# Nine small scale/shift groups, spread key/value tiles and later splits at the start of a two-block kernel

## The chip, the cores and the metric

The kernel runs on one core of one Trainium2 chip. The metric is the device time of one execution in microseconds; a kernel's time is the median of its runs. The engines are named PE (TensorE; PEld is its weight load), ACT (ScalarE), DVE (VectorE), POOL (GpSimd) and SP (SyncE, which issues every DMA here).

## What is computed

Two transformer blocks over 256 tokens of width 2048, all in float32. Only the start of the first matters for the change:

```python
shift, scale, gate = split(silu_c @ w_ada + b_ada, 3)        # w_ada is 2048 x 6144
shift_c, scale_c, _ = split(silu_cc @ w_ada + b_ada, 3)
h  = rmsnorm(x,   norm_g) * (1 + scale)   + shift            # 256 tokens
hc = rmsnorm(ctx, norm_g) * (1 + scale_c) + shift_c          # 256 context tokens
kc, vc = hc @ w_in[:, K and V columns]                       # 8 tiles of 128 columns
p  = h @ w_in                                                # all columns, K and V among them
...                                                          # attention, Fourier mix, merge, second block
```

Every later step needs `h`, and `h` needs the scale and shift rows, which need 4096 columns of `w_ada` (32 MB).

## The kernel before

All operands are feature-major: 16 feature tiles (kt) of 128 partitions, tokens along the free axis. A product of a weight tile with an operand is made of three matmuls in fp32r: the weight is split into a rounded part (`whi`, made by ACT) and the rest (`wlo`, made by DVE), the operand likewise (`act` holds both parts).

Engine queues are recorded by a planner. `Queue.put` adds an instruction and moves the queue's planned time; jobs (generators, in `jobs`) are advanced by `step()` whenever PE's planned time passes the time at which what they wait for is expected, plus `MARGIN`. So the order on ACT and DVE is fixed at build time by planned costs. On the chip only semaphores count, and every engine works its own queue in order.

The work is a `stream` of items, and `flow()` walks it: loads are issued `LOADS` = 8 items ahead into `NR` = 7 raw buffers of 512 KB (SP's DMAs, in stream order; a buffer is loaded again once its last reader is done), weights are split `AHEAD` = 3 items ahead (`prepare`), and then the item's matmuls are put (`piece`). Kinds of item in the start:

- S, a scale/shift tile of `w_ada` (`s_group`, `s_pe`): 512 KB, read raw by four small matmuls of 32 x 256, in the four column groups of PE, with `CW` (the two silu vectors) as weights. Two sections (scale, shift) of a group share one PSUM bank, `s_bank`.
- B, a piece of the first seven of the eight key and value tiles (`together`, `run_group`): some of the seven units, for the feature tiles of one group; `whi`/`wlo` are split from it. Each unit holds a PSUM bank through the whole start, so seven of the eight banks are held, and `s_bank` has the eighth.

`GROUPS` cuts the 16 feature tiles into five groups of 2, 4, 4, 4, 2. When the last S item of a group is through, the job `s_cols` copies the bank (ACT), sums the four row groups with 128x2 matmuls on PE, makes the modulation columns in `mod` (DVE), gives the bank back, and goes on into `h_group`, which makes the operands `act` of the group's feature tiles on ACT and DVE; only then can B items of that group run. A group of n tiles has 16 S items for n = 4 and 8 for n = 2; `S_PLACE` says behind which S items the B items stand. Fifteen of 18 B items stand between S items, three behind them. Then come the eighth value tile (`v7`, two items of kind G), and 24 query and gate tiles and so on, for 2.65 ms.

Before S items, `squares` puts 16 matmuls of ones with x squared, and `norm_in` makes the inverse root from them.

Of the kernel before, what the change touches and what calls it, by code (L numbers as in the profile page):

```python
# [21 lines left out]
S_PLACE = (1, 3), (1, 6), (1, 9), (2, 4), (2, 7), (2, 10), (2, 13), (3, 4), (3, 7), (3, 10), (3, 13), (4, 4), (4, 6), (4, 7), (4, 7)  # L22
KV_FIRST = 7
S_COST = 0.15
# [3 lines left out]
MARGIN = 1.2  # L28
AHEAD = 3
# [89 lines left out]
def block_kernel(nc, src, out):  # L119
# [164 lines left out]

    def hop(tokens):

        if expected(tokens) > PE.time + 0.05:
            yield [(c, v, when - MARGIN) for c, v, when in tokens]

# [66 lines left out]
    def step():  # L356

        moved = False
        for j in list(jobs):
            if j[1] <= PE.time:  # L360
                try:
                    toks = next(j[0])
                    j[1] = expected(toks) + MARGIN if toks else PE.time
                    moved = moved or bool(toks)
                except StopIteration:
                    jobs.remove(j)
                    moved = True
        return moved
# [122 lines left out]
    state = {}  # L491
# [91 lines left out]

    def flow():
        n = len(stream)
        at = 0
        for i in range(-LOADS, n):
# [9 lines left out]
            if 0 <= i + AHEAD < n:  # L597
                prepare(i + AHEAD)
# [33 lines left out]
    GROUPS = ((0, 2), (2, 4), (6, 4), (10, 4), (14, 2))  # L632

    def s_pe(it):
# [3 lines left out]
        n = GROUPS[j][1]  # L638
# [4 lines left out]
        o = bank[:, 256 * sec:256 * sec + 256]  # L643
        w = RAW[it["raw"] % NR]
        PE.wait(it["in"])
        for q in range(4):
            k = q if n == 2 else q // 2
            last = mm(o[32 * q:32 * q + 32, :], CW[:, kts[k], :], w[:, 256 * q:256 * q + 256], kts[0] == 0, kts[-1] == 15,
                      tell=q == 3, cost=S_COST)
# [4 lines left out]
    def s_cols(j, bank, tok):  # L654
# [3 lines left out]
        t = copy(rows[:, :], bank[:, :], tok + f)  # L658
        yield t
        PE.wait(t)  # L660
        for sec in range(2):
            for b in range(n):
                x, sel = (b, 0) if n == 2 else (b % 2, 1 + b // 2)
                at = 2 * (n * sec + b)
                last = mm(bank[:, at:at + 2], rows[:, 256 * sec + 128 * x:256 * sec + 128 * x + 128], col(C_SEL + 2 * sel, 2),
                          True, True, tell=sec == 1 and b == n - 1)
# [499 lines left out]
    def s_group(j):  # L1166
# [7 lines left out]
                       {2: (3, 1, 3), 4: (2, 2, 1, 2)})  # L1174
# [11 lines left out]
    HALVES = (8, 8)  # L1186
    for i in range(KV_FIRST, 8):
# [827 lines left out]
def _lay_out(x):  # L2015
# [36 lines left out]
    for q in range(4):  # L2052
        for at in (C_SEL, C_SEL + 2 + 2 * (q % 2)):
            cols[32 * q:32 * q + 2, at:at + 2] = np.eye(2)
# [20 lines left out]
```

How the kernel before makes its waits and increments, by code:

```python
    def put(self, fn, needs, tell=True, cost=0.1):  # L72
        self.wait(needs)
        self.time += cost
        if not tell:
            self.ops.append(fn)
            return None
        count = self.done
        self.ops.append(lambda e: fn(e).then_inc(count.handle, 1))
        return count.add(1, self.time + self.tail)
# [5 lines left out]
    def play(self, e):  # L86
        for op in self.ops:
            if isinstance(op, tuple):
                e.wait_ge(op[0].handle, op[1])
            else:
                op(e)
# [183 lines left out]
    def dma(o, i, count, needs=(), q=None):  # L275
        q = q or SP
        q.wait(needs)
        q.ops.append(lambda e: e.dma_start(o, i).then_inc(count.handle, 16))
        q.time += max(0.65, size(o) * 4 * 128 / 335e3)
        return count.add(16, q.time + 2.0)
```

## Time and profile before

| | us |
|---|---|
| median of 3 runs | 2834.73 (2834.42 to 2835.02) |
| the profiled execution | 2834.52 |
| its span in the profile | 2832.7 |
| PE busy | 2773.2 (98%) |
| DVE busy | 2077.2 (73%) |
| ACT busy | 1475.7 (52%) |
| HBM read | 612.69 MB, 218 GB/s over the span |

The span is the time from the first to the last instruction that the profiler saw; the device time has 1.8 us more. "Busy" for PE means that a matmul is under way; at half the granted clock a busy PE does half the work. The granted clock is 1.00 at 2.4 GHz and 0.50 at 1.2 GHz. Chain lines, waits and timelines name an instruction by engine, line and tile; buffer numbers are left out, and `[x <-y]` at the end of a line is x us of idle time before it, ended by y.

### The profile page before, as it was taken

What the parts mean: (1) busy time and instruction counts of PE and PEld (TensorE: products, weight loads), DVE (VectorE), ACT (ScalarE), POOL (GpSimd) and SP (SyncE); (2) the same over time, 40 slices, a digit from 0 to 9 for tenths busy, and PEclk for the clock granted to TensorE, in tenths of its full rate; (3) what the DMA queues carried; (4) which work ended last, traced back from release to release, by engine and by line L of the source; (5) the groups of instructions that cost most, each with busy time, mean ns of one, the idle gap of its engine ahead of it and who ended that gap; (6) DMA issues with size and microseconds to landing.
All of it is one profiled execution on the core that took longest, in us unless ns stands there. A gap on an engine that the chain in (4) does not pass through costs nothing. (4 is left out here: it accounts for less than half of the span.)

```text
span 2832.7 us, 43001 instructions
## 1 busy us (share of the span) xinstructions
PE 2773.2 (98%) x16104; PEld 2390.9 (84%) x16104; DVE 2077.2 (73%) x3551; ACT 1475.7 (52%) x2394; POOL 339.6 (12%) x1005
## 2 busy tenths in 40 slices
PE   7899999999989999999999999999989999999999
PEld 3578888888878888888888888888878888888888
DVE  2368877888887888887787877888878765566654
ACT  2265554555557667666666644545444543344443
POOL 0004420000003152423324210000000000000000
PEclk8999999999999999999999999999999999999999
DMA  8866667888955555555555578788768766655554
GB/s 307 287 199 225 212 207 250 284 269 287 314 158 205 175 173 184 168 185 182 171 176 167 169 263 284 252 291 297 251 196 280 246 186 187 193 190 188 185 186 148
DMA packets 196626, 621.82 MB, mean 220 GB/s; under 512 B 20273, under 2 KB 38721, under 8 KB 195649
## 3 DMA queue, kind: packets, MB, share of 16 engines
q1 hardware_dynamic: 196416, 619.08, 66.8%
q8 instruction: 126, 2.06, 0.3%
q14 instruction: 84, 0.68, 0.1%
HBM read 612.69 MB, written 4.21 MB: 218 GB/s over the span
## 5 line engine op out<-in xcount | busy, mean ns | idle before, releaser
L266 PE MATMUL ps<-act,whi 128*128 128x512 f32 x6560 | 1756.8, 399 | 30.3 <-DVE act L261 21.8
L251 DVE TENSOR_TENSOR wlo<-raw,whi 128x1024 fp32r<-128x1024 f32 (+2 forms) x885 | 1045.6, 1186 | 453.3 <-ACT whi L242 252.7
L266 PEld LDWEIGHTS ps<-act,whi 128*128 128x128 f32 x6560 | 1168.5, 189 | 248.0 <-issue 26.8
L242 ACT ACTIVATE whi<-raw 128x1024 fp32r<-128x1024 f32 (+2 forms) x885 | 881.3, 1022 | 210.8 <-PE ps L266 151.0
L266 PE MATMUL ps<-act,wlo 128*128 128x256 f32 (+1 forms) x6416 | 981.4, 287 | 2.3 <-DVE wlo L251 2.3
L266 PEld LDWEIGHTS ps<-act,wlo 128*128 128x128 f32 x6416 | 895.8, 190 | 73.5 <-DVE wlo L251 5.1
L242 ACT ACTIVATE t<-ps 128x256 f32<-128x256 f32 (+2 forms) x393 | 147.9, 377 | 478.3 <-PE ps L266 429.8
L261 DVE SCALAR_TENSOR_TENSOR acc<-raw,c_act,acc 128x1024 f32<-128x1024 f32 x210 | 267.8, 1277 | 0.0
L242 ACT ACTIVATE t<-t 128x256 f32<-128x256 f32 (+3 forms) x261 | 115.5, 443 | 193.5 <-DVE t L251 162.4
L251 POOL TENSOR_TENSOR small<-small 128x2 f32<-128x2 f32 (+2 forms) x460 | 167.0, 363 | 231.3 <-ACT t L242 138.7
L251 DVE TENSOR_TENSOR t<-t,ps 128x256 f32<-128x256 f32 (+2 forms) x391 | 153.8, 394 | 28.1 <-ACT t L242 25.2
L257 POOL TENSOR_SCALAR small<-small 128x2 f32<-128x2 f32 (+3 forms) x256 | 91.1, 356 | 629.2 <-DVE small L257 609.4
L261 DVE SCALAR_TENSOR_TENSOR t<-t,t 128x256 f32<-128x256 f32 (+2 forms) x160 | 70.9, 446 | 25.7 <-ACT t L242 24.2
L266 PE MATMUL ps<-m_act,whi 128*128 128x512 f32 x256 | 64.2, 392 | 0.4 <-ACT whi L242 0.4
L251 POOL TENSOR_TENSOR small<-small,small 128x4 f32<-128x4 f32 (+1 forms) x160 | 57.1, 357 | 13.1
L1443 POOL MEMSET t<- 128x4 f32 x31 | 2.8, 101 | 454.1 <-PE ps L266 420.7
L261 DVE SCALAR_TENSOR_TENSOR h_res<-ps,mod,h_res 128x256 f32<-128x256 f32 x64 | 31.0, 484 | 34.9 <-PE ps L266 33.8
L242 ACT ACTIVATE act<-t 128x256 fp32r<-128x256 f32 x48 | 20.0, 416 | 68.1 <-DVE t L251 68.1
L266 PEld LDWEIGHTS ps<-t,t 128*128 128x128 f32 x286 | 48.4, 189 | 6.8
L266 PE MATMUL ps<-t,t 128*128 128x128 f32 (+1 forms) x286 | 53.9, 281 | 0.0
L266 PEld LDWEIGHTS ps<-m_act,whi 128*128 128x128 f32 x256 | 46.1, 189 | 9.0 <-ACT whi L242 0.6
L251 DVE TENSOR_TENSOR t<-t,t 128x256 f32<-128x256 f32 (+1 forms) x104 | 47.7, 459 | 4.3 <-ACT t L242 1.1
(208 smaller groups left out, 1873.0 us busy)
## 6 DMA issues: line engine op xcount, KB each, us to landing
raw<-in_w SPq DMA_DIRECT2D x427, 512.0 KB, 5.0
raw<-in_w_mod SPq DMA_DIRECT2D x192, 512.0 KB, 4.8
raw<-in_w_ada SPq DMA_DIRECT2D x96, 512.0 KB, 6.4
raw<-in_w_gate SPq DMA_DIRECT2D x88, 512.0 KB, 4.7
raw<-in_w_up SPq DMA_DIRECT2D x88, 512.0 KB, 4.7
raw<-in_w_out SPq DMA_DIRECT2D x64, 512.0 KB, 5.8
raw<-in_w_down SPq DMA_DIRECT2D x64, 448.0 KB, 3.7
raw<-in_p_a SPq DMA_DIRECT2D x32, 512.0 KB, 5.7
```

The source lines that it names most:

```text
L242: return AC.put(lambda e: e.activation(o, i, func, **kw), needs, cost=cost)
L251: return (q or DV).put(lambda e: e.tensor_tensor(o, a, b, op), needs, cost=max(0.4, size(o) * 0.0036) if q else 0.07 + size(o) * 0.00104)
L257: return (q or DV).put(lambda e: e.tensor_scalar(o, a, s1, s2, op0, op1), needs, cost=cost)
L261: return DV.put(lambda e: e.scalar_tensor_tensor(o, a, s, b, op0, op1, **kw), needs, cost=0.07 + size(o) * 0.00104 + 0.06 * column(s))
L266: return PE.put(lambda e: e.matmul(o, w, x, start=start, stop=stop), needs, tell, cost)
L1443: z = GP.put(lambda e: e.memset(xp[:, 0:4], 0.0), f)
```

## The change

1. `GROUPS` has nine groups: two of one feature tile, seven of two. An S item of a one-tile group holds 8 row blocks of 128 columns (512 B runs in HBM) and is read by eight matmuls of 32 x 128; of a two-tile group, 4 row blocks of 256 columns (1 KB runs). The four-tile groups before had 512 columns (2 KB runs). The number of S items stays 64.
2. The B items are 16: one of 7 units in each one-tile group, and two of 4 and 3 units in the others. Their runs are 512 B or 1 KB (1 KB or 2 KB before). `S_PLACE` puts a group's two B items behind the fifth and eighth S item of the group after it; the last two stand behind all S items.
3. In the start a B item is split no earlier than one item ahead of its matmuls (`hasty`), unless the planner expects it to have landed and a `wlo` buffer to be free (`early`). Behind the start (`end_start`) the rule is the old one.
4. Until `end_start` the planner's margin is 0.3 instead of 1.2.
5. `s_cols` copies only the filled part of the bank; the selector columns `C_SEL` lose two variants that the four-tile groups needed.

```diff
-S_PLACE = (1, 3), (1, 6), (1, 9), (2, 4), (2, 7), (2, 10), (2, 13), (3, 4), (3, 7), (3, 10), (3, 13), (4, 4), (4, 6), (4, 7), (4, 7)
+S_PLACE = [(1, 3), (2, 7)] + [(j, p) for j in range(3, 9) for p in (4, 7)]
...
+FIRST_MARGIN = 0.3
...
-            yield [(c, v, when - MARGIN) for c, v, when in tokens]
+            yield [(c, v, when - spare[0]) for c, v, when in tokens]
...
-                    j[1] = expected(toks) + MARGIN if toks else PE.time
+                    j[1] = expected(toks) + spare[0] if toks else PE.time
...
+    def hasty(i, k):
+
+        return state["start"] and k > max(i, 0) + 1 and stream[k]["kind"] == "B"
+
+    def early(it):
+
+        if it["kind"] == "B":
+            return expected(it["in"]) <= PE.time and (ring["hi"] < NL or ("lo", ring["hi"] - NL) in pe_free)
+        return it["kind"] == "S"
...
-            if 0 <= i + AHEAD < n:
-                prepare(i + AHEAD)
+            while after < n and (after <= i + AHEAD and not hasty(i, after) or after < at and early(stream[after])):
+                prepare(after)
+                after += 1
...
-    GROUPS = ((0, 2), (2, 4), (6, 4), (10, 4), (14, 2))
+    GROUPS = [(0, 1), (1, 1)] + [(k, 2) for k in range(2, 16, 2)]
...
-        for q in range(4):
-            k = q if n == 2 else q // 2
-            last = mm(o[32 * q:32 * q + 32, :], CW[:, kts[k], :], w[:, 256 * q:256 * q + 256], kts[0] == 0, kts[-1] == 15,
-                      tell=q == 3, cost=S_COST)
+        for k, kt in enumerate(kts):
+            q = kt % 4
+            last = mm(bank[32 * q:32 * q + 32, c * sec:c * sec + c], CW[:, kt, :], w[:, c * k:c * k + c], kt < 4, kt >= 12,
+                      tell=kt == kts[-1], cost=c / 2330)
...
-        t = copy(rows[:, :], bank[:, :], tok + f)
+        t = copy(rows[:, 0:256 * n], bank[:, 0:256 * n], tok + f)
...
-                       {2: (3, 1, 3), 4: (2, 2, 1, 2)})
+                       {1: (7,), 2: (4, 3)})
...
+    def end_start():
+        spare[0] = MARGIN
+        state["start"] = False
+
+    add({"kind": "X", "run": end_start})
```

On ACT, before: from the column copy of the first group (out of `ps1`) to that of the second (out of `ps2`). `whi` rows are splits of B items, `act` and `t1` rows are `h_group`.

```order
L242 ACTIVATE t2_1_139<-ps1 128x512
L242 ACTIVATE whi0_56<-raw5_54 128x768
L242 ACTIVATE act_65<-xc_66,mod_97 128x256
L242 ACTIVATE t1_1_155<-xc_66,mod_97 128x256
L242 ACTIVATE act_65<-xc_66,mod_97 128x256 x2
L242 ACTIVATE t1_3_157<-xc_66,mod_97 128x256
L242 ACTIVATE act_65<-xc_66,mod_97 128x256
L242 ACTIVATE whi1_57<-raw2_51 128x256
L242 ACTIVATE whi2_58<-raw6_55 128x768
L242 ACTIVATE t2_2_140<-ps2 128x512
```

ACT now, from the copy of the third group to that of the fourth:

```order
L242 ACTIVATE t2_3_141<-ps2 128x512
L242 ACTIVATE act_65<-xc_66,mod_97 128x256
L242 ACTIVATE t1_5_159<-xc_66,mod_97 128x256
L242 ACTIVATE act_65<-xc_66,mod_97 128x256 x2
L242 ACTIVATE t1_7_161<-xc_66,mod_97 128x256
L242 ACTIVATE act_65<-xc_66,mod_97 128x256
L242 ACTIVATE whi2_58<-raw2_51 128x1024
L242 ACTIVATE whi3_59<-raw6_55 128x768
L242 ACTIVATE t2_4_142<-ps2 128x512
```

The operands of a group now stand directly behind its column copy, and the splits behind them; both splits of a group still stand ahead of the next copy.

On PE, before, at the end of the third group (the last matmuls of a B piece, the last two S items, the column sums with `cols`, the first S items of the fourth group; `c_wide` is `CW`):

```order
L266 MATMUL ps1<-act_65,whi1_57 128x512 x2
L266 MATMUL ps1<-act_65,wlo2_63 128x512
L266 MATMUL ps2<-raw3_52,c_wide_92 32x256 x4
L266 MATMUL ps2<-raw4_53,c_wide_92 32x256 x4
L266 MATMUL ps2<-cols_96,t2_3_141 128x2 x8
L266 MATMUL ps2<-raw5_54,c_wide_92 32x256 x4
L266 MATMUL ps2<-raw6_55,c_wide_92 32x256 x4
```

PE now, at the end of the fourth group (feature tiles 4 and 5):

```order
L266 MATMUL ps2<-raw5_54,c_wide_92 32x256 x4
L266 MATMUL ps7<-act_65,whi3_59 128x512 x2
L266 MATMUL ps7<-act_65,wlo3_64 128x512
L266 MATMUL ps7<-act_65,whi3_59 128x512 x2
L266 MATMUL ps7<-act_65,wlo3_64 128x512
L266 MATMUL ps2<-cols_96,t2_4_142 128x2 x4
L266 MATMUL ps0<-act_65,whi3_59 128x512 x2
L266 MATMUL ps0<-act_65,wlo3_64 128x512
```

The column sums stood between S items and now stand inside the B piece of three units, behind its first unit.

## Rows read from the trace of the kernel before

**Rows 1.** The page, part 2: granted clock in tenths, 40 slices.

```profile
PEclk8999999999999999999999999999999999999999
```

**Rows 2.** Busy times by stage: window, length, PE, PEld, DVE, ACT, POOL busy, clock, DMA share, GB/s.

```profile
0.00:183.08 183.08, 152.63 (x948) 99.22 (x949) 64.20 (x144) 60.37 (x104) 0.73 (x5) 0.91 0.81 278
183.08:2832.70 2649.62, 2620.57 (x15157) 2291.71 (x15155) 2012.98 (x3409) 1415.30 (x2291) 338.92 (x1000) 1.00 0.66 215
```

**Rows 3.** Timeline of PE: start, us, what; squares, last S item, first of v7.

```profile
8.32 16.41 PE L266 MATMUL ps<-t,k 128*128 128x512 f32 x32 [8.32 <-ACT t L242]
...
161.97 0.64 PE L266 MATMUL ps<-raw,c_wide 128*32 128x256 f32 x8
...
183.08 1.30 PE L266 MATMUL ps<-act,whi 128*128 128x512 f32 x5
```

**Rows 4.** Timeline of PE: a first product at half clock, S items, products, ones.

```profile
42.07 1.19 PE L266 MATMUL ps<-act,whi 128*128 128x512 f32 x2 [4.42 <-DVE act L251]
...
48.93 1.50 PE L266 MATMUL ps<-raw,c_wide 128*32 128x256 f32 x24
50.36 0.73 PE L266 MATMUL ps<-act,whi 128*128 128x512 f32 x2
...
77.24 0.62 PE L266 MATMUL ps<-act,whi 128*128 128x512 f32 x2
...
77.93 0.62 PE L266 MATMUL ps<-act,whi 128*128 128x512 f32 x2
...
175.88 1.02 PE L266 MATMUL ps<-t,k 128*128 128x512 f32 x2
```

**Rows 5.** Timeline of PE at the end of the third group.

```profile
101.67 1.95 PE L266 MATMUL ps<-cols,t 128*128 128x2 f32 x16 [0.72 <-ACT t L242]
104.72 3.92 PE L266 MATMUL ps<-raw,c_wide 128*32 128x256 f32 x40 [1.10 <-DVE mod L251]
```

**Rows 6.** Busy times in windows of 2 us, before and at a fall of the clock.

```profile
60.00:62.00 2.00, 0.85 (x16) 0.16 (x8) 0.00 (x0) 0.00 (x0) 0.00 (x0) 1.00 1.05 398
...
64.00:66.00 2.00, 1.78 (x9) 1.78 (x10) 0.00 (x0) 0.17 (x1) 0.00 (x0) 0.60 1.06 389
```

**Rows 7.** The same windows where the queues are full or empty.

```profile
10.00:12.00 2.00, 2.00 (x4) 0.78 (x3) 0.69 (x1) 1.15 (x2) 0.00 (x0) 1.00 1.03 434
12.00:14.00 2.00, 2.00 (x5) 0.92 (x4) 0.69 (x1) 0.33 (x1) 0.00 (x0) 1.00 0.98 413
...
24.00:26.00 2.00, 2.00 (x29) 0.82 (x31) 0.69 (x1) 0.51 (x1) 0.00 (x0) 1.00 0.30 96
...
46.00:48.00 2.00, 2.00 (x8) 1.60 (x7) 0.14 (x1) 0.00 (x0) 0.00 (x0) 0.66 0.00 0
```

**Rows 8.** Waits of SP's queue in 0 to 200 us (us, times, longest); landing of raw tiles.

```profile
SPq L278 <- PE ps L266: 107.2, 47, 10.1
...
DMA to landing us min/median/max: 2.5/6.5/15.6
```

**Rows 9.** ACT's waits for landings; timeline of ACT and DVE around the first operands.

```profile
ACT whi L242 <- DMA raw<-in_w: 50.7, 11, 9.5
...
37.11 0.84 ACT L242 ACTIVATE whi<-raw 128x768 fp32r<-128x768 f32 x1 [6.84 <-DMA raw<-in_w]
...
38.93 0.15 DVE L251 TENSOR_TENSOR mod<-ps,cols 128x2 f32<-128x2 f32 x1
...
42.41 0.99 DVE L251 TENSOR_TENSOR act<-t,act 128x256 fp32r<-128x256 f32 x2 [0.49 <-ACT t L242]
```

**Rows 10.** Rates: 1 KB rows, 2 KB rows, and stretches with key/value loads.

```profile
16.00:24.00 8.00, 8.00 (x20) 3.60 (x19) 2.08 (x3) 2.54 (x3) 0.00 (x0) 1.00 1.10 348
62.00:68.00 6.00, 4.24 (x28) 3.51 (x24) 0.27 (x3) 0.60 (x1) 0.00 (x0) 0.70 1.05 388
90.00:104.00 14.00, 12.63 (x91) 8.85 (x89) 1.53 (x4) 1.65 (x2) 0.00 (x0) 1.00 0.98 348
126.00:130.00 4.00, 3.62 (x34) 2.13 (x32) 0.00 (x0) 1.00 (x1) 0.00 (x0) 1.00 0.95 262
126.00:142.00 16.00, 13.09 (x102) 9.18 (x104) 2.60 (x9) 2.33 (x4) 0.00 (x0) 1.00 1.02 320
```

More of the change, by code:

```diff
@@ L21 @@
 HEADS = 5
-S_PLACE = (1, 3), (1, 6), (1, 9), (2, 4), (2, 7), (2, 10), (2, 13), (3, 4), (3, 7), (3, 10), (3, 13), (4, 4), (4, 6), (4, 7), (4, 7)
+S_PLACE = [(1, 3), (2, 7)] + [(j, p) for j in range(3, 9) for p in (4, 7)]
 KV_FIRST = 7
-S_COST = 0.15
 V_LATE, Z_LATE = 1, 1
@@ L283, in lo_part @@
         return tt(o, full, hi.bitcast(F32), ALU.subtract, needs)
+    spare = [FIRST_MARGIN]
     def hop(tokens):
         if expected(tokens) > PE.time + 0.05:
-            yield [(c, v, when - MARGIN) for c, v, when in tokens]
+            yield [(c, v, when - spare[0]) for c, v, when in tokens]
     def split(kt, s, full, needs, scale=1.0):
@@ L489, in prepare @@
             state[key] = t + u
-    state = {}
+    state = {"start": True}
     def piece(it):
@@ L582, in run_group @@
         pe_free[("hi", n)] = pe_free[("lo", n)] = last
+    def hasty(i, k):
[4 more added lines that the diff above has]
+        return it["kind"] == "S"
     def flow():
         n = len(stream)
-        at = 0
+        at = after = 0
         for i in range(-LOADS, n):
@@ L629, in act_c @@
         t1.give(big, toks)
-    GROUPS = ((0, 2), (2, 4), (6, 4), (10, 4), (14, 2))
+    GROUPS = [(0, 1), (1, 1)] + [(k, 2) for k in range(2, 16, 2)]
     def s_pe(it):
         sec, j, kts = it["sec"], it["j"], it["kts"]
-        n = GROUPS[j][1]
+        c = 128 * GROUPS[j][1]
         if kts[0] == 0 and sec == 0:
@@ L642, in s_pe @@
         bank = state["s_bank"]
-        o = bank[:, 256 * sec:256 * sec + 256]
         w = RAW[it["raw"] % NR]
         PE.wait(it["in"])
-        for q in range(4):
-            k = q if n == 2 else q // 2
-            last = mm(o[32 * q:32 * q + 32, :], CW[:, kts[k], :], w[:, 256 * q:256 * q + 256], kts[0] == 0, kts[-1] == 15,
-                      tell=q == 3, cost=S_COST)
+        for k, kt in enumerate(kts):
+            q = kt % 4
+            last = mm(bank[32 * q:32 * q + 32, c * sec:c * sec + c], CW[:, kt, :], w[:, c * k:c * k + c], kt < 4, kt >= 12,
+                      tell=kt == kts[-1], cost=c / 2330)
         raw_free[it["raw"]] = state["acc", 0] = last
@@ L662, in s_cols @@
             for b in range(n):
[L663 to L666, printed above, removed]
+                x = n * sec + b
+                last = mm(bank[:, 2 * x:2 * x + 2], rows[:, 128 * x:128 * x + 128], col(C_SEL, 2), True, True,
+                          tell=sec == 1 and b == n - 1)
         t2.give(rows, last)
@@ L2052, in _lay_out @@
     for q in range(4):
-        for at in (C_SEL, C_SEL + 2 + 2 * (q % 2)):
-            cols[32 * q:32 * q + 2, at:at + 2] = np.eye(2)
+        cols[32 * q:32 * q + 2, C_SEL:C_SEL + 2] = np.eye(2)
     cols[:, C_EPS], cols[:, C_E2] = EPS, EPS * EPS
```

## The prediction

> **What bounds the kernel now.** First the page: TensorE is busy in 98% of the span, and the only one of 40 slices in which its granted clock is below nine tenths is the first [rows 1]. Then the busy times by stage: I cut at 183.08 us, where the first matmuls of the eighth value tile (v7) start, since the edited part of the program ends there [rows 2, 3]. Up to that cut PE is idle for 183.08 − 152.63 = 30.5 us, the granted clock is 0.91 and the queues move 278 GB/s; behind it PE is idle for 29 us in 2649.6, at clock 1.00. The end is therefore PE's: whatever the start gives back, the rest keeps, if its order stays. It does: after the start the engines' orders differ by a few interleaved rows only.
>
> What PE must do before the cut, at the full clock: until 24.66 us the load wait and the 32 squares matmuls; 64 scale/shift tiles at 0.48 us (three in 1.43, from 48.93 to 50.36); 112 tile products of keys and values at 0.684 us (spacing 77.24 to 77.93); column sums of 32 blocks, 8 take 1.95 us, so 7.8; two matmuls with ones, some 0.85 each, 1.7 [rows 3 to 5]. 24.7 + 30.7 + 76.6 + 7.8 + 1.7 = **141.5 us**. The other 42 us are 22 us of idle behind 8.32 and matmuls at the half clock. Where they are: at the end of each of the three big groups PE waits 0.72 us for ScalarE's copy of the columns, sums, and waits 1.10 us for VectorE's modulation columns, since seven of eight banks are held by key and value tiles and the next group's first matmul needs the eighth [rows 5]. Around that, tiles come one by one and the clock falls to 0.50 [rows 6]. While PE then runs a burst of key/value products, the 7 raw buffers are full and the queues stand still, 0 GB/s at 46 to 48 us [rows 7]; SyncE's queue waited 107.2 us for PE in the first 200 [rows 8]. And ScalarE blocks in its order on the split of a tile that has not landed: 6.84 us before 37.11, behind which stood the modulation that the operands needed (DVE 38.93) [rows 9].
>
> **The change, part by part.** I follow two floors, the queues' and PE's, to the moment at which v7 starts.
>
> *Row lengths.* The tile bytes stay the same: 64 × 512 KB, 7.34 MB of key/value weights, k1 0.92 MB. Their runs get shorter. Before: 10.2 MB in 1 KB rows, 30.7 MB in 2 KB rows. After: 5.11 MB in 512 B rows (8 tiles and 2 of 448 KB), 35.8 MB in 1 KB rows. Rates: x in 8 KB rows 413 to 434 GB/s; 1 KB rows 348; 2 KB rows 388 [rows 7, 10]. A row then takes one of 16 engines 47.1 ns for 1 KB and 84.5 for 2 KB, that is 9.7 + 37.4 per KB; for 512 B this gives 28.4 ns, 288 GB/s (an extrapolation; bounds 348, no penalty, and 174, same time per row). These are rates without key/value loads in the stream. With them 2 KB rows made 348 over 14 us, and a mixed stretch of mostly 1 KB rows 320 over 16 us, with 262 in its first 4 us, behind a key/value load [rows 10]. I take 320 for the mixed 1 KB stream.
>
> The Trainium skill, "DMA: Bandwidth & Descriptors", section Specifications, gives 512 B as the least transfer at line rate. By it the shorter rows would cost nothing; the rows above show 348 against 388 already from 2 KB to 1 KB, and nothing here shows 512 B. At 388 for all, the 129.5 us of the next paragraph would be 105.4.
>
> *Queue floor.* x is in at 14.0 us. 5.11 MB at 288: 17.7. 35.8 MB at 320: 111.8. k1 at about 430: 2.1. Sum 145.6. Behind the last scale/shift tile stand only 1.31 MB of key/value tiles and k1, 6.2 us, so that tile is transferred at 139.4 and landed at about 140.6 (the shortest way of a tile from issue to landing took 2.5 us, [rows 8], of which some 1.4 are its transfer). Holes: before, tile 8 could not be issued before PE was through the squares, a hole behind 24 us, 96 GB/s in the window [rows 7]; now the slower 512 B rows fill it (7 tiles take 12.7 us, to 26.7). One hole remains, I think: the first key/value piece cannot start before it is landed and split (about 33 us), runs some 7 us since the clock will have fallen, as it had by 42 us before, and holds all seven buffers: 2 us. Later groups: a period is 8 tiles and 7 tile columns × 2, 5.1 MB, 16 us at 320, against 8 × 0.48 + 0.95 + 14 × 0.684 = 14.4 us of PE. PE's longest piece is 8 products, 5.5 us, against 7 buffers, about 11 us. That is enough cover, with small holes of 0.3 us a group: 2 us in all. Last tile then at 144.6.
>
> *Tail.* From the last scale/shift matmul: 0.5; then the copy, 0.7, beside one unit of the 3-unit piece, 1.4 (the order rows on PE show it ahead of the sums), sums 0.95, modulation 0.9, and from there 3.7 us to the second tile of operands (39.7 to 43.4 before, [rows 9]): 7.0; then 13 products 8.9, ones 1.7: 18.1 us (20.6 before, from 162.5 to 183.08, [rows 3]). The piece of group 7 (4.1 us) lies beside the chain, as group 3's did. So v7 at 162.7 by the queues.
>
> *PE floor.* 141.5, plus 3.5 idle until the first piece, 2.5 before the second, 4 at half clock, 1 to 2 in the tail, 0.3 × 6: 155. The 0.72 and 1.10 us waits, and 1.95 of sums with nothing beside them, go: after the third group the sums stand inside a piece, and the bank is read long before the next group needs it. The four more column copies, 0.6 us each on ScalarE, are hidden: ScalarE is busy for 60 of 183 us [rows 2]. The 512 B tiles take 8 matmuls of 128 columns instead of 4 of 256: 0.48 to 0.96 us each, 0 to 4 us, hidden, since PE waits for loads there. PE joins at 155, the queues at 163, so the queues decide; I add 1.3 for half-clock stretches in which PE falls behind. **v7 at 164, 19.1 us earlier.**
>
> *Splits only once landed, margin 0.3.* They move 50.7 us of ScalarE waits for DMA [rows 9] behind the copies and operands. Worth what the chains above assume; by themselves nothing. What is late next is the last piece of each group: ScalarE still splits it ahead of the column copy (the order rows on ACT), and it lands 1.2 us after the last tile: up to 2 us a group when PE is level with the loads. With 2.5 us between chain and use I count none of it.
>
> *After the cut* nothing is added: ±2 us of interleaving.
>
> Total, against the profiled execution's own 2834.5: 2815.4. The median of the runs is 2834.73, 0.2 above, so **2815.6**. Faster or slower than 0.2% (5.7 us) is about what a measurement of this kernel can tell.
>
> **The rivals.**
> (A) The short rows cost little in the mixed stream (348, as without key/value loads; by the page's rule more still): 35.8 MB take 102.9 us, 9 less, and PE's 155 decides: 25 to 32 us gained, 2807. For it: 348 over 90 to 104 us with key/value loads, if in 2 KB rows. Against: 262 at 126 to 130, right behind a key/value load [rows 10].
> (B) PE's clock falls in each group. The tiles come 1.6 us apart for 0.48 us of work, and just such a stretch stood before the clock's fall at 64 us (0.85 us busy of 2 at 60 to 62, clock 0.60 at 64 to 66) [rows 6]. Each costs 2.3 us (4.7 us of work at half clock, from 42.07 to the middle of the window from 46 us, clock 0.66, [rows 4, 7]); seven of them 16, of which the 1.6 us of slack a group hides part: 7 to 12 us lost, gain 7 to 12, 2825. Against: PE is then late, has a backlog and runs without gaps. The Trainium skill, "TensorE: Matmul & The Clock Gate", section on HAM oscillation, tells of this: a wait for loads in each tile puts each tile at the half clock. By it this case would be the rule; here I see it as the second likeliest.
> (C) The change doesn't do what it says: the split is put where the planner expects the landing, at 335 GB/s, and the stream comes at 288 to 320. Then copy and operands wait behind it, 2 us × 7 = 14: gain 5, 2830.
> (D) Slower: the key/value loads in 1 KB rows hold the whole stream at the 262 GB/s of 126 to 130 us. 35.8 MB take 136.6 us, 24.8 more than I count: v7 at 189, 2840. It decides from 273 GB/s, where v7 stands at 183.
>
> **How the numbers follow.** Forecast (gain 13 to 25) 0.50, A 0.18, B 0.18, C 0.08, D 0.06. The range holds the forecast, A, and most of B: 2803 to 2827. Faster by over 0.2%: forecast, A and most of B, 0.83; within: C and the rest of B, 0.11; slower: D, 0.06.
>
> **What would show it.** v7's first matmul at 164 (155 for A, 174 for B). Rates of 340 to 350 (20 to 26 us in 512 B rows: 288) and no stretch at 0 GB/s after 45 us. No wait of PE for modulation columns after the second group. PE idle before the cut near 20 us. If v7 comes as said and the total does not, the rest of the order was not neutral; if 512 B rows run at 348, my line through two row lengths was wrong; if the clock is under 0.9 before the cut, B was right.

## The result and the profile after

| | before | after |
|---|---|---|
| median of 11 runs each, side by side (us) | 2835.59 (2833.14 to 2838.24) | 2828.92 (2826.89 to 2831.01) |
| profiled execution: span, its run (us) | 2832.7, 2834.5 | 2828.2, 2830.0 |
| v7's first matmul (us) | 183.08 | 176.57 |
| from there to the end of the span (us) | 2649.6 | 2651.6 |

The ratio is **0.9975, interval 0.9966 to 0.9984**: 6.7 us faster. The forecast was 19 us and a range from 2803 to 2827. The sign was right, the size a third of what I said, and the time is above my range. v7 should have started at 164.

On the page the busy share of TensorE is 98% as before, and the row of granted clocks is the same to the digit as in [rows 1]; at this grain the two kernels can't be told apart:

```profile
PE 2769.7 (98%) x16168; PEld 2393.1 (85%) x16168; DVE 2080.4 (74%) x3573; ACT 1477.8 (52%) x2396; POOL 339.3 (12%) x1005
PEclk8999999999999999999999999999999999999999
```

The busy times of the changed kernel, cut at v7's first matmul (columns as in [rows 2]; clock, DMA share and GB/s are the last three):

```profile
0.00:176.57 176.57, 145.89 (x1012) 98.89 (x1013) 66.76 (x161) 60.90 (x103) 0.73 (x5) 0.93 0.88 286
176.57:2828.20 2651.63, 2623.78 (x15157) 2294.16 (x15155) 2013.63 (x3413) 1416.89 (x2293) 338.55 (x1000) 1.00 0.66 215
```

TensorE's idle time ahead of the cut went from 30.5 to 30.7 us. What the change won there is busy time (152.6 us before, 145.9 now), and most of it is matmul time at the half clock: the granted clock stood at 0.50 for 34 of the 183 us before and for 24 of the 177 now, and busy time weighted by the granted clock, half-microsecond by half-microsecond, went only from 138.8 to 136.8 us. The timeline of TensorE tells where the idle time is now: the first matmuls of the first, second, fourth and following pieces, the last scale/shift tiles, the sums, the last piece, and v7:

```profile
35.92 1.19 PE L266 MATMUL ps<-act,whi 128*128 128x512 f32 x2 [3.45 <-DVE act L251]
48.50 0.64 PE L266 MATMUL ps<-raw,c_wide 128*32 128x256 f32 x8 [1.64 <-DMA raw<-in_w_ada]
52.55 1.19 PE L266 MATMUL ps<-act,whi 128*128 128x512 f32 x2 [3.41 <-ACT whi L242]
...
62.63 2.37 PE L266 MATMUL ps<-raw,c_wide 128*32 128x256 f32 x40
64.93 0.74 PE L266 MATMUL ps<-act,whi 128*128 128x512 f32 x2
...
81.18 0.70 PE L266 MATMUL ps<-act,whi 128*128 128x512 f32 x2 [1.07 <-ACT whi L242]
98.40 0.70 PE L266 MATMUL ps<-act,whi 128*128 128x512 f32 x2 [1.76 <-ACT whi L242]
114.39 0.70 PE L266 MATMUL ps<-act,whi 128*128 128x512 f32 x2 [0.53 <-ACT whi L242]
131.04 0.70 PE L266 MATMUL ps<-act,whi 128*128 128x512 f32 x2 [1.16 <-ACT whi L242]
148.95 0.70 PE L266 MATMUL ps<-act,whi 128*128 128x512 f32 x2 [0.85 <-ACT whi L242]
155.42 1.50 PE L266 MATMUL ps<-raw,c_wide 128*32 128x256 f32 x24
158.34 0.95 PE L266 MATMUL ps<-cols,t 128*128 128x2 f32 x8
164.37 0.70 PE L266 MATMUL ps<-act,whi 128*128 128x512 f32 x2 [2.24 <-ACT whi L242]
176.57 2.88 PE L266 MATMUL ps<-act,whi 128*128 128x512 f32 x12
```

The waits for column copies and modulation of [rows 5] are gone: the sums stand inside a piece and nothing waits for VectorE's columns. In their place TensorE waits for ScalarE's split at the first piece of every group. From the third piece (64.93) to the eighth group's first piece (148.95) a group takes 84.02 / 5 = **16.80 us**; the single groups take 16.25, 17.22, 15.99, 16.65 and 17.91 us, and in the last of them the granted clock was at 0.50 from 132.5 to 136.5 us. The third piece is late, too.

The queues in six stretches, one in 512 B rows, three in 1 KB rows, two in which next to nothing moves:

```profile
18.00:20.00 2.00, 2.00 (x6) 0.94 (x5) 0.69 (x1) 0.95 (x3) 0.00 (x0) 1.00 1.18 294
42.00:44.00 2.00, 2.00 (x16) 1.34 (x18) 1.63 (x3) 0.00 (x0) 0.00 (x0) 1.00 0.02 7
54.00:56.00 2.00, 2.00 (x7) 1.62 (x7) 0.00 (x0) 0.00 (x0) 0.00 (x0) 0.50 1.10 348
62.00:64.00 2.00, 2.00 (x32) 1.07 (x34) 2.00 (x3) 0.16 (x1) 0.00 (x0) 1.00 0.00 0
84.00:86.00 2.00, 2.00 (x11) 1.65 (x10) 0.00 (x0) 0.61 (x1) 0.00 (x0) 1.00 1.07 355
88.00:90.00 2.00, 2.00 (x28) 1.20 (x18) 0.00 (x0) 0.60 (x1) 0.00 (x0) 1.00 0.63 175
```

Where nothing holds the queues they make about 350 in two-tile groups, also with key/value loads among the tiles, not 320; over the five groups they make 309, holes included. They stand still behind the first two bursts of products and slow down behind the later ones (175 GB/s above, 90 at 138 to 140 us at the lowest). SyncE's queue shows why (issues from 88 to 100 us; the second number is how long it was at them):

```profile
88.33 1.47 SPq L278 DMA_DIRECT2D raw<-in_w_ada  x2
89.85 0.51 SPq L278 DMA_DIRECT2D raw<-in_w  x1
90.46 5.43 SPq L278 DMA_DIRECT2D raw<-in_w_ada  x3
```

and from the view of the transfers of the same stretch, the time from issue to landing of a key/value piece:

```profile
raw<-in_w SPq DMA_DIRECT2D x1, 512.0 KB, 7.3
```

The eight products from 81.18 on end at 87.6. The group's last three tiles have landed and stand behind them on TensorE. Only when TensorE has read the first of them, at about 88.2, is there a buffer for the loads that follow. The next group's first piece is issued at 89.85 and has landed 7.3 us later, at 97.2; behind it stands its split, and TensorE, which waits for that, goes on at 98.40.

Behind the cut the changed kernel loses 2.0 us. The loss lies close to it: from v7 to the first matmul of m_act (the operand of the matmuls from 714 us on) it takes 537.9 us instead of 533.0, and TensorE has a stall that before has not:

```profile
196.66 1.11 PE L266 MATMUL ps<-act,wlo 128*128 128x256 f32 x8
200.74 0.85 PE L266 MATMUL ps<-act,whi 128*128 128x512 f32 x2 [2.96 <-ACT whi L242]
```

### The profile page after: what moved, and what is told of

It is laid out like the page before. It is cut to its first block and busy times, and to the rows that moved or that the text cites. A ratio compares the mean times of both kernels' runs of the same rounds, so it can differ in the third digit from the quotient of the medians.

```text
span 2828.2 us, 43167 instructions
## 1 busy us (share of the span) xinstructions
PE 2769.7 (98%) x16168; PEld 2393.1 (85%) x16168; DVE 2080.4 (74%) x3573; ACT 1477.8 (52%) x2396; POOL 339.3 (12%) x1005
## 5 line engine op out<-in xcount | busy, mean ns | idle before, releaser
L266 PE MATMUL ps<-act,whi 128*128 128x512 f32 x6560 | 1759.2, 400 | 34.8 <-DVE act L261 16.9
L251 POOL TENSOR_TENSOR small<-small 128x2 f32<-128x2 f32 (+2 forms) x460 | 162.8, 354 | 231.5 <-ACT t L242 138.8
```

The costliest lines, as they stand in the source:

```text
L251: return (q or DV).put(lambda e: e.tensor_tensor(o, a, b, op), needs, cost=max(0.4, size(o) * 0.0036) if q else 0.07 + size(o) * 0.00104)
L266: return PE.put(lambda e: e.matmul(o, w, x, start=start, stop=stop), needs, tell, cost)
```

## The experiments

All times are of profiled executions unless a median is named; ratios are to runs of the kernel before on the same chip. Twelve kernels ran. "Third piece" is its first product (64.93 in the changed kernel); the period is that of the two-tile groups (of the changed kernel over five groups, else over the last four; over the last four the changed kernel's is 16.9).

How far single executions can be compared: e7 has the changed kernel's order on TensorE and ScalarE up to about 168 us, and yet its third piece came at 66.53 instead of 64.93, its seventh group's at 134.56 instead of 131.04, and v7 1.7 us later; 1.2 us of that is a later first scale/shift tile (26.26 instead of 25.07). Over all kernels this tile, which every one of them has in the same place, started between 24.12 and 26.26 us. A difference of some 2 us in v7 between two executions tells nothing by itself. Nor is a profiled execution always a typical one: e1's was 4.2 us below its median, e11's 5.9 us.

| kernel | third piece | period | v7 | v7 to end | median | ratio |
|---|---|---|---|---|---|---|
| before | – | – | 183.08 | 2649.6 | 2835.6 | 1 |
| after | 64.93 | 16.8 | 176.57 | 2651.6 | 2828.9 | 0.9975 |
| e1 eight buffers | 61.84 | 16.0 | 169.00 | 2646.6 | 2821.6 | 0.9950 |
| e3 old split rule | – | – | 176.90 | 2659.6 | 2839.0 | 1.0009 |
| e4 old groups, new rule | – | – | 181.00 | 2651.5 | 2833.5 | 0.9990 |
| e5 pieces of 3, 2, 2 | – | 18 to 19.6 | 189.39 | 2648.1 | 2838.7 | 1.0008 |
| e6 before, eight buffers | – | – | 175.74 | 2651.6 | 2830.1 | 0.9985 |
| e7 swaps by ScalarE | – | 17.0 | 178.31 | 2648.7 | 2827.6 | 0.9970 |
| e8 e5 + e7 + eight buffers | – | 18 to 19.6 | 184.72 | 2649.4 | 2835.7 | 1.0004 |
| e9 warm start | 60.70 | 16.0 | 169.03 | 2651.6 | 2821.8 | 0.9951 |
| e10 warm start, eight buffers | 61.59 | 16.0 | 167.91 | 2647.6 | 2819.2 | 0.9942 |
| e11 six buffers | 66.18 | 18.0 | 184.78 | 2651.9 | 2844.6 | 1.0027 |
| e12 e10 + halved splits | 60.30 | 15.46 | 165.21 | 2648.4 | 2815.6 | 0.9932 |

### e1: one raw buffer more

```diff
-NR, NH, NL = 7, 5, 4
+NR, NH, NL = 8, 5, 4
```

> The changed kernel with eight raw buffers instead of seven (and four small tiles of work space fewer, 10 instead of 14). Ring theory: in the changed kernel a group lasts 16.7 us because a burst of eight products keeps all seven buffers, the next group's tiles 4 and 5 and its first piece are then issued together, and the piece lands 6 to 7 us later; one more buffer lets one more tile of 1.5 us be on its way, so a group shortens by 1 to 1.5 us, and v7 starts at 166 to 170 instead of 176.6. Queue theory (the mixed stream cannot be faster) and clock theory: v7 stays at 175 to 178. The total may move otherwise, since later stages get fewer small tiles.

Median 2821.59, ratio 0.9950 (0.9933 to 0.9966). The changed kernel has four small temporaries fewer with it, 10 instead of 14. The first product with wlo of two groups:

```profile
94.27 0.50 PE L266 MATMUL ps<-act,wlo 128*128 128x512 f32 x1 [1.12 <-DVE wlo L251]
110.27 0.50 PE L266 MATMUL ps<-act,wlo 128*128 128x512 f32 x1 [1.12 <-DVE wlo L251]
```

and the busy times of one whole group:

```profile
108.40:124.40 16.00, 14.88 (x118) 10.42 (x114) 6.43 (x18) 5.45 (x9) 0.00 (x0) 1.00 0.99 323
```

The wait for the first half of the split is gone and groups come every 16.00 us: 14.88 of work and 1.12 of waiting for the split's second half, wlo. v7 starts 7.6 us earlier. So the eighth buffer was worth 7.6 us in the changed order (3.1 of it before the third piece, though the clock was at 0.50 in the first two bursts as in the changed kernel). That is not yet a proof that the change itself ran into them (see e6).

### e2: a third of each product

In the start each product of a key/value tile does one matmul of its three (the hi-by-H one) and leaves two out; planned costs are kept, so that the order stays.

```diff
-                mm_hi(u, hi[:, w], x, kt == 0, needs + it["hi"])
-                last = mm_lo(u, lo[:, w], x, kt == 15, it["lo"], kt == it["kts"][-1])
+                if u.width == 512:
+                    last = mm(u.out, hi[:, w], x[1], kt == 0, kt == 15, needs + it["hi"] + it["lo"], ...)
```

> The changed kernel with the same order on every engine, but of each key/value product in the start only the rounded-by-rounded matmul is run, so a burst of eight products takes 1.8 us instead of 5.5 (the other two thirds of these products are left out of the computation). Ring theory: the buffers come back early, the queues run without holes at about 350 GB/s, the last scale/shift tile is in at about 132 us and v7 starts at 143 to 148. Queue theory with my 320 GB/s: last tile at 141, v7 at 153 to 156. If the stream of loads alone makes the 16.7 us a group: v7 at 165 or later.

One run, 2809.34. The last scale/shift tiles begin at 139.46:

```profile
136.08 3.44 PE L266 MATMUL ps<-act,whi 128*128 128x512 f32 x8 [3.38 <-DVE wlo L251]
139.46 1.50 PE L266 MATMUL ps<-raw,c_wide 128*32 128x256 f32 x24
```

They end at 141.0; the changed kernel does it at 156.9. The forecast said 145.1, of which 4 us were holes: its floor alone is 141.1. With short bursts the queues keep to that floor, so it was not too low; what was wrong is to expect that the real order reaches it. The ring theory's own numbers were missed, though (last tile in at 132, v7 at 143 to 148): the last tile, and v7 at about 156, came where the queue theory with 320 GB/s had them. The rate was not 320 but 337 GB/s from 59 to 139 us; the third piece came at 59.33, and the groups took 15.1 us, with TensorE waiting for splits in each (3.38 us above). So e2 shows that long bursts cost the real order 16 us at the last tile, and not that the ring is all of it.

### e3 and e4: the two halves of the change

```diff
 e3: the changed kernel
-        return state["start"] and k > max(i, 0) + 1 and stream[k]["kind"] == "B"
+        return False
...
-            return expected(it["in"]) <= PE.time and (...)
+            return False
```

> The changed kernel (nine groups, spread pieces, margin 0.3) with the old rule for splits, three items ahead. If the later splits are worth what they move, ScalarE waits again on loads ahead of the column copies, and v7 comes 5 to 10 us later than 176.6. If the ring of buffers sets the pace, an early placed split frees its buffer as soon as it is landed and costs nothing: v7 at 174 to 178.

v7 at 176.90, as in the changed kernel: the late splits give nothing in the start that one execution could show. The median is nevertheless 2839.0, ratio 1.0009 (1.0000 to 1.0019), 10 us above the changed kernel's. Between the two profiled executions it is 8.3 us, and 8.0 of them arise behind the cut: e3 needs 2659.6 us from v7, against 2651.6. One such place is near 820 us; first TensorE in the changed kernel, then in e3:

```profile
818.41 0.77 PE L266 MATMUL ps<-act,whi 128*128 128x512 f32 x1 [1.96 <-DVE act L261]
```

```profile
821.44 0.77 PE L266 MATMUL ps<-act,whi 128*128 128x512 f32 x1 [4.62 <-DVE act L261]
```

The same wait costs 2.7 us more. I did not find out what in the start sets this off; I only show where it is.

e4 is the other half: the groups and places of before, with the new rule for splits and the margin of 0.3.

```diff
-    GROUPS = [(0, 1), (1, 1)] + [(k, 2) for k in range(2, 16, 2)]
+    GROUPS = ((0, 2), (2, 4), (6, 4), (10, 4), (14, 2))
```

> The kernel before (five groups, its 18 pieces and their places) with the new split rule and the margin 0.3. If the gain of 6.5 us before v7 comes from the groups and the spread pieces: v7 stays at 181 to 184 and the time within 0.1% of before. If it comes from the splits: v7 at 176 to 178.

v7 at 181.00, median 2833.53, ratio 0.9990 (0.9981 to 0.9999). Of the 6.5 us in the start the rule with the margin gives 2.1, which is no more than two executions of one order can differ by, and groups and margin without the rule give 6.2 (e3). The gain there belongs to the groups; the margin was not tried alone.

### e5: shorter bursts

```diff
-S_PLACE = [(1, 3), (2, 7)] + [(j, p) for j in range(3, 9) for p in (4, 7)]
+S_PLACE = [(1, 3), (2, 7)] + [(j, p) for j in range(3, 9) for p in (2, 4, 7)]
...
-                       {1: (7,), 2: (4, 3)})
+                       {1: (7,), 2: (3, 2, 2)})
```

> The seven key/value units of a two-tile group come as pieces of 3, 2 and 2 behind tiles 2, 4 and 7, instead of 4 and 3 behind 4 and 7; nothing else is changed, and the products are all there. Theory (a ring of seven raw buffers): a burst of 8 products, 5.5 us, holds every raw buffer, and what is freed at its end lands 6 to 7 us later; a group takes 16 to 17.9 us. With bursts of 6, 4 and 4 products the longest is 1.4 us shorter, so a group takes about 15.3 us, TensorE's waits of 0.5 to 1.8 us at the first piece of a group shrink below 0.6, and v7 starts at about 167 us instead of 176.6. Rival 1 (the stream's rate, or the waits for the splits, set the group): three late splits a group instead of two, group 16.7 us or more, v7 at 176 to 180. Rival 2 (TensorE's clock falls more often with shorter bursts): granted clock before the cut under 0.90 (0.93 in the changed kernel), v7 at 174 or later. The total follows v7 by plus or minus 5 us, since the order behind the cut moves.

v7 at 189.39, median 2838.68, ratio 1.0008 (0.9999 to 1.0017): against the theory, and worse than rival 1. TensorE and ScalarE around one first piece:

```profile
99.89 0.70 PE L266 MATMUL ps<-act,whi 128*128 128x512 f32 x2 [1.96 <-ACT whi L242]
```

```profile
95.96 0.60 ACT L242 ACTIVATE act<-xc,mod 128x256 fp32r<-128x256 f32 x1 [2.63 <-DVE mod L251]
98.92 0.83 ACT L242 ACTIVATE whi<-raw 128x768 fp32r<-128x768 f32 x1
```

(The first fence is TensorE, the second ScalarE.) Sums, modulation, operands and then the split of the first piece are one chain. In the changed kernel five tiles stand between the last piece's products and the first of the next group; here three, and the last piece is a unit shorter. TensorE runs out of work ahead of the chain's end, some 2.5 us a group, and then has a third piece whose load takes a buffer (11 loads a group through seven buffers instead of 10). The clock has a part in it, too. It was at 0.50 for some 4 us in three of the last four groups, once in the changed kernel; the group without such a stretch and one with it (columns as in [rows 2]):

```profile
119.50:137.55 18.05, 15.56 (x115) 10.24 (x115) 6.40 (x18) 5.65 (x10) 0.00 (x0) 1.00 0.88 285
137.55:157.19 19.64, 17.16 (x114) 11.38 (x115) 6.39 (x18) 5.65 (x10) 0.00 (x0) 0.91 0.80 259
```

So the chain alone makes 18.05 us, and a stretch at the half clock costs another 1.6. Rival 2 is true in part: the clock fell more often, though its mean before the cut is 0.91 and not under 0.90. e5 changed the chain and the number of loads with the burst, and tells nothing on the length of bursts alone.

### e6: the kernel before with eight buffers

The edit is e1's, on the kernel before (temporaries as in e1).

> The kernel before with eight raw buffers instead of seven (and ten small temporaries instead of fourteen). It asks whether the eighth buffer needs the changed order to be worth something. Theory (the ring limits the changed order, while the kernel before is limited by the chain from the last tile of a big group to its modulation columns, for which the next group waits): v7 at 179 to 182 instead of 183.1, total within 4 us of the kernel before. Rival (the eighth buffer is worth 7 us in either order): v7 at about 176, total 2828.

v7 at 175.74, median 2830.06, ratio 0.9985 (0.9976 to 0.9994). The rival was right: the eighth buffer gives 7.3 us in the old order and 7.6 in the new. And the change gives 6.7 us with eight buffers (175.74 to 169.00), 6.5 with seven. The two gains add. The seven buffers are no new bound that the change ran into. They were a cost of the old order too, which my sum, made of floors, had counted as gone.

### e7: the key jobs' swaps issued by ScalarE

```diff
-        sw = swap_halves(ks[:, 0:256], kg[:, 0:256], cnt, c + f + fc)
+        sw = swap_halves(ks[:, 0:256], kg[:, 0:256], cnt, c + f + fc, q=AC)
```

It is meant for the stall at 200.74. There SyncE's queue was held from 171.1 to 179.1 us by the third key job's swap, with weight loads behind it, and nothing moved meanwhile. The changed kernel's busy times, and SyncE's queue:

```profile
176.00:178.00 2.00, 2.00 (x11) 1.65 (x10) 1.97 (x7) 0.08 (x1) 0.00 (x0) 1.00 0.00 0
178.00:180.00 2.00, 2.00 (x10) 1.44 (x8) 1.16 (x2) 1.97 (x4) 0.00 (x0) 1.00 0.00 0
```

```profile
170.55 0.58 SPq L278 DMA_DIRECT2D raw<-in_w_ada  x1
179.13 1.10 SPq L278 DMA_DIRECT2D t<-t  x2
```

> The changed kernel with the key jobs' eight small transfers (swapping the halves of a tile) issued by ScalarE, right behind the copy that makes their source, instead of by SyncE's queue. Theory (what the changed kernel gives back behind the cut is this: SyncE stood from 170.6 to 179.1 us at the third key job's swap with the weight loads queued behind it, nothing moved from 174 to 180 us, the splits came late, TensorE stood 2.96 us at 200.74 and then ran at 0.79 of the clock): v7 unchanged at 176 to 177, no stretch of 6 us at 0 GB/s, no stall at 200, and m_act's first split 533 to 534 us behind v7 instead of 537.9; total some 4 to 5 us lower, about 2824. Rival (the loss of 4.9 us is spread over the interleaving, and one stall only takes another's place): m_act 537 to 539 us behind v7, total 2827 to 2831.

The hole is filled in part (81 GB/s from 176 to 180), but a stall of 2.07 us stands at 195.96, again for the split, and m_act's first matmul comes 537.5 us behind v7. The rival was right in this: one stall took another's place. Ratio 0.9970 (0.9960 to 0.9980), not to be told from the changed kernel's.

### e8: shorter bursts, eight buffers, swaps

> The changed kernel with all three: pieces of 3, 2 and 2, eight raw buffers, and the key swaps issued by ScalarE. Theory (ring): a group is now limited by the stream alone, 5.1 MB at about 350 GB/s, 14.6 us, or by TensorE's 14.4; seven groups 1.4 us shorter than with eight buffers alone (v7 at 169.0): v7 at 159 to 161, and, with 2646 us from there as with eight buffers, a span of 2806 and a run at about 2809. Rival (eight buffers and shorter bursts take away the same wait and don't add): v7 at 166 to 169, run at 2814 to 2818.

v7 at 184.72, ratio 1.0004 (0.9994 to 1.0013), outside both. It agrees with e5: a group takes 18.04 us at the full clock (115.36 to 133.40) and 19.6 with a stretch at the half clock (133.40 to 153.00), as with seven buffers, so neither buffers nor swaps shorten the chain.

### e9: a warm start

```diff
+    def warm(count):
+        bank = state.get("kv")
+        if bank is not None:
+            for _ in range(count):
+                mm(bank[0:30, 0:256], CW[:, 0, 2:32], K1[:, 0:256], False, False, cost=0.001)
+            return
+        bank, free = banks.free[-1]
+        PE.wait(free)
+        for _ in range(count):
+            mm(bank[:, 0:256], ident, K1[:, 0:256], True, True, cost=0.001)
...
+        if state["start"] and it["kts"][0] < 2:
+            warm(8)
...
+        if (j, sec, kts[0]) == (1, 1, 0):
+            warm(5)
+        if j == 2 and (sec, kts[0]) != (0, 0):
+            warm(4 if (sec, kts[-1]) == (1, 15) else 1)
```

> The changed kernel, in which TensorE gets 32 matmuls of 128x256 floats more (constants against the identity into a free bank, or against zero weights into a key bank): 5 ahead of the second group's fifth tile, 8 ahead of the first key/value piece, 1 ahead of most tiles and 4 ahead of the last tile of the third group, 8 ahead of the second piece. They fill the idle time from 29 to 36 and from 46 to 52.5 us; every other instruction stands in the same order. Theory (a good part of what the forecast missed lies before 65 us: the clock at one half from 31 to 41 and from 51 to 61 us makes the first two bursts of 7 products take 7.7 and 9 us instead of 4.8, and nothing is transferred at 42 to 46 and 60 to 64 us meanwhile): clock 1.00 in both bursts, the third piece's first product at 58 to 61 us instead of 64.9, v7 at 170 to 173 instead of 176.6. Rival 1 (the early loads set the pace: what the bursts win, the wait for the next tile and split loses): third piece at 64 to 65, v7 at 176 to 177. Rival 2 (the added matmuls are themselves in the way, each 0.43 us): v7 at 177 to 180.

Median 2821.79, ratio 0.9951 (0.9937 to 0.9966). First the changed kernel from 36 to 44 and from 52 to 60 us, then e9:

```profile
36.00:44.00 8.00, 8.00 (x33) 6.25 (x37) 3.40 (x12) 1.59 (x3) 0.00 (x0) 0.70 0.69 220
52.00:60.00 8.00, 7.46 (x21) 5.89 (x22) 2.93 (x10) 2.73 (x6) 0.00 (x0) 0.50 1.08 346
```

```profile
36.00:44.00 8.00, 8.00 (x63) 5.67 (x62) 3.19 (x12) 1.59 (x3) 0.00 (x0) 1.00 0.80 248
52.00:60.00 8.00, 8.00 (x64) 5.80 (x66) 3.68 (x14) 4.01 (x7) 0.00 (x0) 1.00 0.70 223
```

31 matmuls that compute nothing (the expectation counts 32) made the program 7 us faster. With them the granted clock is 1.00 in both bursts (0.50 from 52 to 60 before), the third piece starts at 60.70, 4.2 us earlier, and the groups behind it come every 16.0 us although there are seven buffers. The theory holds, beyond its number (169.0, said 170 to 173). The loads do come earlier: the second piece has landed, and ScalarE splits it, 3.6 us sooner (first the changed kernel, then e9).

```profile
51.45 0.95 ACT L242 ACTIVATE whi<-raw 128x896 fp32r<-128x896 f32 x1 [9.48 <-DMA raw<-in_w]
```

```profile
47.88 0.95 ACT L242 ACTIVATE whi<-raw 128x896 fp32r<-128x896 f32 x1 [7.69 <-DMA raw<-in_w]
```

Of the 3.3 us that e9 gains between the third piece and the eighth group's first, about 1.6 is the stretch at the half clock that the changed kernel has there and e9 has not. For the rest I suppose that loads which lag when the two-tile groups begin cost the later groups too; no run shows this alone.

### e10: warm start and eight buffers

> The same added matmuls with eight raw buffers instead of seven. Theory (two separate causes, which add): v7 at 169.0 with eight buffers alone, less what the warm start gives with seven, so 163 to 166, which is what the forecast had said; total 2812 to 2818. Rival (with eight buffers the stream no longer stops in the slow bursts, so a warm start has nothing to give): v7 at 168 to 170, total as with eight buffers alone, 2821.

v7 at 167.91, ratio 0.9942 (0.9926 to 0.9959), which can't be told from e1's or e9's. The rival: each alone gives some 7.5 us, both together 8.7, so they run into the same limit. That limit stands in the timeline, at the same distance each time:

```profile
110.74 0.50 PE L266 MATMUL ps<-act,wlo 128*128 128x512 f32 x1 [1.11 <-DVE wlo L251]
126.73 0.50 PE L266 MATMUL ps<-act,wlo 128*128 128x512 f32 x1 [1.12 <-DVE wlo L251]
```

### e11: six buffers

The edit is e1's, with 6 (and 18 small temporaries).

> The changed kernel with six raw buffers. Theory (a ring: the time of a group is set by how long the buffers stay held by the tiles behind a burst, and one buffer fewer lets each load start one tile later, 1.5 us): a group takes 17.5 to 18.5 us instead of 16.8, v7 at 183 to 188 instead of 176.6. Rival (the ring binds only in the start-up, before 65 us): groups of 16.5 to 17 us and v7 at 178 to 180.

Median 2844.56, ratio 1.0027 (1.0018 to 1.0037); v7 at 184.78, the wait for the split at a first piece up to 1.9 us:

```profile
120.87 0.70 PE L266 MATMUL ps<-act,whi 128*128 128x512 f32 x2 [1.88 <-ACT whi L242]
155.58 0.70 PE L266 MATMUL ps<-act,whi 128*128 128x512 f32 x2 [1.79 <-ACT whi L242]
```

Six buffers 18.0 us a group (83.51 to 155.58 in four), seven 16.8, eight 16.0: the ring theory's numbers, and not the rival's. With six as with seven, one of these groups holds a stretch at the half clock (104 to 107.5 us); the other three take 17.7 us, and the changed kernel's other four 16.5. And 16.8 is not fixed by the number seven: e9 has 16.0 with it.

### e12: the split in halves

```diff
+            cut = [0, c // 2, c] if kind == "B" and c == 1024 else [0, c]
+            for x, y in zip(cut, cut[1:]):
+                h = copy(hi[:, x:y], raw[:, x:y], ...)
+                l = lo_part(lo[:, x:y], raw[:, x:y], hi[:, x:y], ...)
+                it["halves"].append((y, h, l))
...
+                h, l = next((h, l) for y, h, l in it["halves"] if at < y)
```

> The kernel with eight buffers and the added matmuls, in which a four-unit piece is split in two halves (ScalarE copies 512 columns, VectorE subtracts them, then the other 512), and a product waits for its own half alone. Orders on TensorE and ScalarE are otherwise the same. Theory (with both causes gone a group is a loop of 16.00 us on TensorE and the chain columns, modulation, operands, split: 14.88 us of work and a wait of 1.12 us for the second half of the split, wlo): the wait goes, the first product starts 0.5 us earlier, and a group takes 14.9 to 15.2 us, which is also what the stream can do (5.2 MB at 350 GB/s); v7 at 161 to 164 instead of 167.9, total 2811 to 2816. Rival (the loads bind first, since the stream only made 321 to 328 GB/s over these groups with eight buffers): groups of 15.7 to 16, a wait for DMA or for the split behind it in place of the one for wlo, v7 at 166 to 168, total 2817 to 2821.

Median 2815.61, ratio 0.9932 (0.9915 to 0.9948): the lowest median, though the interval overlaps those of e1, e9 and e10. The wait for wlo is 0.58 us instead of 1.12, and a group takes 15.46 us:

```profile
107.29 0.50 PE L266 MATMUL ps<-act,wlo 128*128 128x512 f32 x1 [0.58 <-DVE wlo L251]
122.75 0.50 PE L266 MATMUL ps<-act,wlo 128*128 128x512 f32 x1 [0.58 <-DVE wlo L251]
```

That is between theory and rival. The loads were not the bound: ScalarE splits the first piece right behind the group's operands, without waiting for a landing.

```profile
104.31 0.59 ACT L242 ACTIVATE act<-xc,mod 128x256 fp32r<-128x256 f32 x1
104.81 1.14 ACT L242 ACTIVATE whi<-raw 128x512 fp32r<-128x512 f32 x2
```

The five groups are 2.7 us shorter than e10's. That v7 comes 2.7 us earlier than e10's is in part chance, for e12's first scale/shift tile started 1.6 us earlier, and its tail, with the clock at 0.50 from 152.5 to 156.5 us, took 1.3 us longer. v7 at 165.21 and the total of 2815.6 are where I had forecast the changed kernel, with three edits that it lacks.

## Why the prediction was wrong

**The rows: right where they were extrapolated, too slow where they were read.** 512 B rows made 286 to 294 GB/s, I had said 288. 1 KB rows with key/value loads made 348 to 355 where nothing held them, not 320. The 262 of [rows 10], on which rival D hung, was part of a hole, I now think: the changed kernel shows values below 300 in this stream only beside a burst. No run tests it. A's condition (348 in the mixed stream) held, without A's result. The Trainium skill, "DMA: Bandwidth & Descriptors", section Specifications, gives 512 B as enough for line rate; the 294 against 350 here disagree.

**The step that failed: the holes in the queue floor, 2 us in the start and 0.3 us a group, the latter since "PE's longest piece is 8 products, 5.5 us, against 7 buffers, about 11 us. That is enough cover".** I compared the length of a burst with the bytes in the ring. But three of the seven buffers hold landed tiles that stand behind the burst, and what is issued when they come free is back 7.3 us later, with its split behind it. It is a loop, not a store, and e11, after and e1 show what a buffer is worth in it: 18.0, 16.8 and 16.0 us a group with six, seven and eight. A group's 5.11 MB take 14.6 us at 350 GB/s, so the holes and waits are 2.2 us a group, not 0.3. That the group of 16.3 in the forecast looks nearly right is luck: the rate was put too low (16.0 us at 320 GB/s) by most of what the holes were. The old order pays for having only seven buffers as well (7.3 us there, 7.6 here), and I set a sum for the new order, which had next to nothing for it, against a measured time of the old one, which had it in full. So a cost of both orders was counted as gained.

**The start is the larger part, 8.3 us.** Working back from my 145.1 for the end of the last scale/shift tile (7.0 for the burst and three tiles, five groups of 16.3) the third piece stood at 56.6; it came at 64.93. I had allowed one hole of 2 us ("One hole remains, I think"); the queues stood nearly still from 42 to 46 and from 60 to 64. I had priced the half clock at 4 us on TensorE's own floor and at nothing on the queues', since I took the two floors as separate. They are coupled through the buffers: a slow burst holds them longer. e9 shows the coupling, since work that keeps TensorE at its full clock makes the loads come earlier. But it explains 4.2 of the 8.3 us, and the eighth buffer alone 3.1; with both (e10, e12) the third piece still came at 61.59 and 60.30, 4 to 5 us behind the sum. What these are stays open. Behind the third piece the sum is: five groups at 16.8 for 16.3, 2.5 us; from the last group's burst to its last tile 1.0; tail and half clock 19.65 for 18.9, 0.75. With 8.3 that is 12.55 us, 164 to 176.57, and about 1.6 of the five groups' time is the one stretch at the half clock.

**A new wait in place of the old.** The waits for copy and modulation went, as said. I wrote that the last split of a group, ahead of the copy, might cost up to 2 us and counted none. What stood in the way was the first piece's split, behind the operands: 0.5 to 1.8 us and 0.54 for wlo in each group, 2.24 us in the tail, and 1.12 us even with all else mended (e1, e10), half of which e12 takes.

**The rivals.** B said 2825 and a gain of 7 to 12, and part of its reason is in the result. Its place was wrong: the clock fell in the two one-burst groups at the beginning (31 to 41 and 51 to 61 us), where e9 shows the price, and only once (132.5 to 136.5 us) in the five groups, whose mean granted clock was 0.98. B's price of 2.3 us a fall was too high: e5's groups with and without one differ by 1.6. And B's condition was not met: in these groups the tiles did not come one by one, but TensorE read five in 2.37 us and three in 1.50 without a gap, as B's own "against" had it. The Trainium skill, "TensorE: Matmul & The Clock Gate", section on HAM oscillation, tells of a wait for loads in each tile; this trace has none there, so it neither bears the page out nor speaks against it. C's number (2830) is the nearest, but its mechanism is not what happened: it had copy and operands wait behind the split, and the trace shows the split behind the operands; e3, with the old rule for splits, has v7 at the same place.

**Behind the cut.** "±2 us of interleaving" is nearly right: eleven of the twelve executions in the table with all products took 2646.6 to 2651.9 us from v7 to the end, 3.0 less to 2.3 more than the 2649.6 before (two of them, e1 and e11, ran 4 and 6 us faster than their medians, so their typical time may lie higher); e3 with 2659.6 is out by 10. The changed kernel's own loss of 2.0 us is in it. Why e3's order is so much worse stays open; e7 moved the stall nearest to the cut, and the time didn't change.

## What to carry to other kernels

Do not hold two floors (queues, TensorE) side by side when a ring of buffers couples them: follow one buffer through its loop, from the issue past what stands ahead of its tile on the engine, and price the loop per buffer. Ask whether TensorE's clock is at the half just ahead of a long burst, behind idle time: here 31 matmuls that compute nothing paid there. And when one limit is lifted, look at once for the next: here the eighth buffer and the warm start each gave some 7.5 us, both together 8.7, and the next limit was the split behind the operands.

## What the runs showed of the hardware

- Rows of 512 B moved at 286 to 294 GB/s, 1 KB rows at 348 to 355, 2 KB rows at 388 [rows 10]: the line through the time per row, drawn through the last two, held for the first.
- Under a full queue a 512 KB load had landed 7.3 us after its issue (89.85 to 97.2 us), against 2.5 us for the shortest before [rows 8].
- A stretch of some 4 us at 0.50 of the clock within a group made the group 1.6 us longer (19.64 against 18.05 us, e5).
- 31 matmuls of 128x256 floats with no use, 1 to 8 in a row between real ones, held the granted clock at 1.00 (2.4 GHz) from 28 to 68 us, where it had been 0.50 (1.2 GHz) in two stretches.
